# Two-layer RWKV-7/GLA decoder step: decays moved between the v tiles, the norm over heads in two token halves, identity products in the routings

## The chip, the cores and the metric

The kernel runs on one core of one Trainium2 chip. The metric is the device time of one execution in microseconds, as the median of several runs. Everything is float32 apart from a few bf16 0/1 matrices in the routing.

## The reference, cut to what matters

264 token rows (256 of a prompt, 8 samples of one token each) pass two layers. Layer 0 mixes with RWKV-7 (12 heads of 64), layer 1 with gated linear attention. Beside each mixer runs a small cross-attention to 256 memory tokens, and behind each a hierarchical mixture of 32 experts, of which each token uses two. The change concerns layer 0's mixer and the step from either mixer into its experts:

```python
w_log = -softplus(-(w0 + tanh(xw @ w1) @ w2)) - 0.5
decay = exp(-exp(w_log))
def step(S, inp):                       # per token; S is (head, value, key)
    sa = einsum('bhij,bhj->bhi', S, -kk_t)
    S = S * d_t[:, :, None, :] + sa[..., None] * b_t[:, :, None, :] + v_t[..., None] * k_t[:, :, None, :]
    return S, einsum('bhij,bhj->bhi', S, r_t)
mean = mean(y, -1); var = mean(square(y - mean), -1)     # per token and head
gn = ((y - mean) * rsqrt(var + GN_EPS)) * ln_g + ln_b
bonus = sum(r4 * k4 * r_k, -1) * v4
out = (gn + bonus) * g
...
x = x + mixed @ w_out
x = x + hier_moe(rms_norm(x, norm_ffn_g), ...)           # scores, top group, top 2 experts, SwiGLU experts
```

## The kernel before, in words

Each engine has its own program, and all order between engines is by semaphores that the code counts by hand. Within an engine the order is the order of the code. `link` makes an engine wait for its own instruction before the next; `mark` does this with a semaphore that others read as well (`t_dve`, `t_act`).

Layer 0's mixer (`mixer0` in each engine's program). The features stand on partitions, the tokens in columns, 128 features (two heads, a "pair") to a tile, six tiles to a vector. PE multiplies the input by the weights of r, k, v and of the low-rank gates, tile by tile, into two PSUM banks in turn; ACT copies each tile out (`out`). The last two weight chunks are those of r (`columns(4, ...)`) and of v (`columns(5, (512, 256))`, four and two tiles). After the v tiles PE sums r·k·r_k over each head (`head_sums(TT[0], 2)`), DVE forms the exclusive decay (`T2 = vL - vld`, L1828), ACT takes the exponentials into `TT[2]`, `TT[1]` and `TT[0]` (L1350 to L1354), DVE multiplies the head sums with v into `vld` (L1832) and scales r, kk, k and b (L1837 to L1840). `TT[2]` is also what the v products read, `TT[0]` what the head sums read. PE starts the scan at `T_SCALED`.

The scan handles 256 tokens as four chunks of 64, in two halves of two chunks. `scan_steps()` writes the order of its steps as a list, which PE, ACT and DVE all go through: each step is one group of 64x64 products into one of six banks (L857, L854), then one copy by ACT (L1379) or one masked copy or addition by DVE (L1883, names in `ON_DVE`). For each half a triangular matrix is inverted in steps (N, NT, X2, U1, ... U5); the chain (RHS, SA, Z, Y) then carries the state over the chunks, and Y's copy puts the scan's output into `vL`. The first half's chain lies among the second half's inversion; the second half's chain ends the scan. Between these, DVE updates the eight samples' states in 18 `sample_step`s (L1856 to L1872), one behind every second step of its own from the 16th on. Their result goes through memory (SP, L428 and L430) and comes back as `Dn[0]`, which PE transposes.

The norm over heads follows when the scan has ended and the samples are there: head sums of y (L767, six products of 264 columns into six banks), centring by DVE (L1916), square (L1918), head sums again, logarithm and exponential by ACT (L1387, L1388) for the inverse root, and five products or sums by DVE (L1920 to L1924) into `mixedT`. `t_dve` 9 ends it. SP waits for it and for the stored prompt state before it issues the first expert weights; the two chunks of `w_out` it has issued before.

`output` multiplies `mixedT` by `w_out` (L754), adds x by products with the identity (L757), forms router scores (L738) and transposes back (L742); `finish` is the second part for one tile. `route` on DVE then scales the scores, finds groups and experts, and builds one-hot matrices; PE counts ranks in between (L1154, L1159) and then gathers the tokens of the first four experts (L1064), whose units of 2 MB of weights it multiplies next (L1083). Weights run through a ring of eight units, in order, on SP's queue (L367); SP issues unit n when PE has used unit n - 8, units 6 and 7 of each layer when the two `w_out` halves are read.

Of the kernel before, what the change touches and what calls it, by code (L numbers as in the profile page):

```python
# [15 lines left out]
D = 1024  # L16
# [59 lines left out]
def scan_steps():  # L76
# [17 lines left out]
    return steps + fill + [(1, *c) for c in CHAIN]  # L94
# [3 lines left out]
SCAN = [st for st in STEPS if st[1] != "D"]  # L98
# [15 lines left out]
T_STATE_OUT = 4  # L114
# [21 lines left out]
T_MIXED = [9, 13]  # L136
OUT_STORES = [2, 4]
SEMS = """consts x_loaded norm_ss norm_h hT_ps hT gain_loaded router_w
# [14 lines left out]
def build(nc, A, O, dbg=None):  # L153
    with ExitStack() as ctx:
# [166 lines left out]
        Dn = [mixedT.rearrange("p k t -> p (k t)")[0:TS, TOK * n:TOK * (n + 1)] for n in range(2)]  # L321
        Dn += [h.rearrange("p t d -> p (t d)")[0:TS, TOK * n:TOK * (n + 1)] for n in range(4)]
        dscr = nc.dram_tensor("sample_vectors", [6, TS * TOK], F32, kind="Internal").ap()
# [46 lines left out]
        def _(sp):  # L370
# [32 lines left out]
            def mixer0():  # L403
# [26 lines left out]
                sp.dma_start(Dn[0], yscr.rearrange("(b c) -> b c", b=TS)).then_inc(s["dec_y"], 16)  # L430
                for i in range(2):
                    load_chunk(lambda b: [k3(b[:, 0:KT * 512], KT)], [A["w_out"][0].rearrange("(k p) n -> p k n", p=128)[:, :, 512 * i:512 * (i + 1)]])
# [167 lines left out]
        def _(pe):  # L600
# [128 lines left out]

            def output(l):  # L730
# [31 lines left out]
                finish(KT - 1)  # L762

            def head_sums(src, n):

                for q in range(PAIRS):
                    last = pe.matmul(ps[2 + q][:, 0:T], block64[:, :], src[:, q, :], start=True, stop=True)  # L767
                last.then_inc(s["sum_ps"], 1)

            def mixer0():  # L770
# [32 lines left out]
                columns(5, (512, 256))  # L803
                pe.wait_ge(s["t_dve"], 3)
                head_sums(TT[0], 2)

                def sample_rows(n):

                    src = (TT[2], vr, vk, vv, vkk, vb)[n]
# [51 lines left out]
                for st in STEPS:  # L861
                    if st[1] == "D":
                        sample_rows(st[2])
                    else:
                        scan_step(st)
                for st in SCAN[-BANKS:]:
                    wait_out(st)
                for q in range(PAIRS):
                    for u in range(2):
                        rows = slice(C * u, C * (u + 1))  # L870
                        last = pe.matmul(ps[2][rows, C * q:C * (q + 1)], cZ[rows, 0, q, :], ident[rows, rows], start=True, stop=True)
                last.then_inc(s["qn_ps"], 1)

                pe.wait_ge(s["dec_y"], 32)
                for q in range(PAIRS):
                    last = pe.transpose(ps[4][:, TS * q:TS * (q + 1)], Dn[0][:, 128 * q:128 * (q + 1)], ident[0:TS, 0:TS])
                last.then_inc(s["qn_ps"], 1)
                pe.wait_ge(s["t_act"], T_STATE_OUT)
                pe.wait_ge(s["t_act"], 5)
                head_sums(vL, 3)  # L880
                pe.wait_ge(s["t_dve"], 8)
                head_sums(TT[1], 4)
                pe.wait_ge(s["t_dve"], 9)

            def mixer1():
# [164 lines left out]
                for q in range(PAIRS):  # L1050
                    if q == 0:
                        pe.wait_ge(s["t_dve"], 10)
# [88 lines left out]
            for l in range(DEPTH):  # L1141
# [18 lines left out]
                last.then_inc(s["rank_ps"], 1)  # L1160

# [51 lines left out]
        def _(act):  # L1213
# [113 lines left out]
            def mixer0():  # L1327
# [17 lines left out]
                for dst in (vr, vv):  # L1345
                    for q in range(PAIRS):
                        out(dst[:, q, :], 128)

                act.wait_ge(s["t_dve"], 4)
                act.activation(TT[2][:, 0:PAIRS, TP:T], vld[:, :, TP:T], ACT.Exp)  # L1350
                act.activation(TT[2][:, 0:PAIRS, 0:TP], TT[2][:, 0:PAIRS, 0:TP], ACT.Exp)
                act.activation(TT[1][:, 0:PAIRS, 0:TP], vL[:, :, 0:TP], ACT.Exp).then_inc(s["t_act"], 1)
                act.wait_ge(s["t_dve"], 5)
                act.activation(TT[0][:, 0:PAIRS, 0:TP], vL[:, :, 0:TP], ACT.Exp, scale=-1.0).then_inc(s["t_act"], 1)  # L1354
# [4 lines left out]
                for st in STEPS:  # L1359
                    half, name, hf = st  # L1360
                    c = 2 * half + hf
                    if name == "D":
# [3 lines left out]
                        last.then_inc(s["qn"], 1)  # L1366
                    elif name not in ON_DVE:
# [13 lines left out]
                act.copy(cKn[:, 0], ps[2][:, 0:384].rearrange("p (q n) -> p q n", q=PAIRS)).then_inc(s["t_act"], 1)  # L1381
                act.wait_ge(s["qn_ps"], 9)
                act.copy(vL[:, :, TP:T], ps[4][:, 0:TS * PAIRS].rearrange("p (q b) -> p q b", q=PAIRS)).then_inc(s["t_act"], 1)

                act.wait_ge(s["sum_ps"], 4)
                for q in range(PAIRS):
                    link(act.activation(TT[1][:, q, :], ps[2 + q][:, 0:T], ACT.Ln, scale=1.0 / 64, bias=cst[:, 2:3]))  # L1387
                act.activation(TT[1][:, 0:PAIRS, :], TT[1][:, 0:PAIRS, :], ACT.Exp, scale=-0.5).then_inc(s["t_act"], 1)  # L1388
# [174 lines left out]
        def _(dve):  # L1563
# [209 lines left out]
            def mixer0():  # L1773
# [53 lines left out]
                dve.wait_ge(s["pj_out"], 43)  # L1827
                mark(dve.tensor_tensor(T2[:, :, 0:TP], vL[:, :, 0:TP], vld[:, :, 0:TP], ALU.subtract), "t_dve", 4)  # L1828
                dve.wait_ge(s["sum_ps"], 2)
                dve.wait_ge(s["t_act"], 2)  # L1830
                for q in range(PAIRS):
                    link(dve.tensor_tensor(vld[:, q, :], ps[2 + q][:, 0:T], vv[:, q, :], ALU.mult))  # L1832
                mark(dve.memset(sq[:, 0:1], 0.0), "t_dve", 5)
                dve.wait_ge(s["t_act"], 3)
                pc = slice(0, TP)
                link(dve.tensor_copy(lam[:, :, :], T1[:, :, C - 1:TP:C]))
                link(dve.tensor_tensor(vr[:, :, pc], vr[:, :, pc], T1[:, :, pc], ALU.mult))  # L1837
                link(dve.scalar_tensor_tensor(out=vkk[:, :, pc], in0=vkk[:, :, pc], scalar=-1.0, in1=T2[:, :, pc], op0=ALU.mult, op1=ALU.mult))
                link(dve.tensor_tensor(vk[:, :, pc], vk[:, :, pc], T0[:, :, pc], ALU.mult))
                mark(dve.tensor_tensor(vb[:, :, pc], vb[:, :, pc], T0[:, :, pc], ALU.mult), "t_dve", 6)  # L1840
# [33 lines left out]

                done_d, sampled = 0, 0
                for st in SCAN:
                    half, name, hf = st
                    if name not in ON_DVE:
# [26 lines left out]
                    mark(last, "c_dve", c_at(st))  # L1905
                    done_d += 1
# [7 lines left out]
                dve.wait_ge(s["sum_ps"], 3)  # L1914
                for q in range(PAIRS):
                    link(dve.scalar_tensor_tensor(out=T0[:, q, :], in0=ps[2 + q][:, 0:T], scalar=-1.0 / 64, in1=vL[:, q, :], op0=ALU.mult, op1=ALU.add))  # L1916
                mark(dve.memset(sq[:, 0:1], 0.0), "t_dve", 7)
                mark(dve.tensor_tensor(T1, T0, T0, ALU.mult), "t_dve", 8)  # L1918
                dve.wait_ge(s["t_act"], 6)
# [177 lines left out]
```

## Time and profile before

| what | value |
|---|---|
| three timed runs | 1717.71, 1719.99, 1725.26 us; median 1719.99 |
| profiled execution | 1716.36 us, span 1714.3 us |
| PE, DVE, ACT busy | 75%, 24%, 14% of the span |
| mean granted TensorE clock | 0.847 of full speed |
| DMA | 463.62 MB, mean 270 GB/s |

```profile
PEclk9968889897888998798998889779698888786686
DMA  9410202043659999999999823318399999999994
```

The span is cut into 40 slices of 42.9 us. A digit is a slice's mean in tenths: of the TensorE clock that was granted, and of the busy share of the 16 DMA engines. The two long runs of 9 in the second line are the experts of the two layers.

### The profile page before, as it was taken

The page shows a single profiled execution, that of the slowest core. Times are in us where ns is not written, and L with a number is a line of the kernel's source. Part 1 is how long each engine was busy: PE and PEld are TensorE (multiplying, and loading weights), DVE is VectorE, ACT ScalarE, POOL GpSimd, SP SyncE. Part 2 cuts the span into 40 slices and gives each one's busy share as a digit, 9 for nine tenths or more (in the row PEclk, how much of TensorE's full clock was granted, in tenths as well). Part 3 has the DMA queues.
Part 4 walks back from the last instruction along what each step waited for, and adds up shares of the span by engine and source line. Part 5 has one row for each costly group of instructions (what it writes and reads, how often), then busy time and mean ns, then how long its engine had stood idle before and what let it go on. Part 6 is the DMA issues. An engine that isn't in the chain of part 4 may idle for free.

```text
span 1714.3 us, 20945 instructions
## 1 busy us (share of the span) xinstructions
PE 1289.6 (75%) x9284; PEld 695.7 (41%) x9284; DVE 412.4 (24%) x824; ACT 246.4 (14%) x653; POOL 18.0 (1%) x53
## 2 busy tenths in 40 slices
PE   2968967775796775696675799879788665969774
PEld 1556757774651221332131466548433211514311
DVE  4044645853211110110110232430211011011013
ACT  2110322121210000010000222412100000101001
POOL 1000000000000000000000000000000000000000
PEclk9968889897888998798998889779698888786686
DMA  9410202043659999999999823318399999999994
GB/s 301 135 50 25 74 1 46 3 139 140 257 231 409 409 409 409 408 409 409 409 409 401 260 76 87 128 44 338 139 410 409 409 409 408 408 409 409 409 409 173
DMA packets 147457, 463.62 MB, mean 270 GB/s; under 512 B 12850, under 2 KB 37188, under 8 KB 147164
## 3 DMA queue, kind: packets, MB, share of 16 engines
q1 hardware_dynamic: 145964, 457.78, 69.3%
q0 software_dynamic: 1392, 4.38, 0.8%
q8 instruction: 77, 1.26, 0.3%
q14 instruction: 24, 0.20, 0.0%
HBM read 455.12 MB, written 7.02 MB: 270 GB/s over the span
## 4 chain that ended last, share of the span: by engine, by line
PE 48%; DMA 34%; DVE 9%; issue 3%; ACT 3%; SPq 3%; DVEq 0%; ACTq 0%
DMA slot<-in_exp_w_up 23%; PE bank L1083 9%; PE bank L1064 7%; PE bank L640 6%; DMA arena<-in_exp_w_up 6%; DMA slot<-in_exp_w_down 6%; PE bank L754 4%; PE bank L857 3%; PE bank L898 3%; PE bank L904 3%; SPq L367 2%; PE bank L1094 2%; PE bank L726 1%; PE bank L659 1%; DVE arena L1883 1%
## 5 line engine op out<-in xcount | busy, mean ns | idle before, releaser
L1083 PE MATMUL bank<-slot,hT 128*32 128x512 f32 x1536 | 238.4, 741 | 127.7 <-DMA slot<-in_exp_w_up 127.6
L1083 PEld LDWEIGHTS bank<-slot,hT 128*32 128x32 f32 x1536 | 49.9, 125 | 301.3 <-DMA slot<-in_exp_w_up 172.4
L1668 DVE SCALAR_TENSOR_TENSOR mixedT<-mixedT,bank 128x512 f32<-128x512 f32 x16 | 11.0, 687 | 523.9 <-ACT mixedT L1238 523.9
L1083 PE MATMUL bank<-slot,mixedT 128*32 128x512 f32 x768 | 100.0, 664 | 35.5 <-DMA slot<-in_exp_w_down 28.7
L1083 PE MATMUL bank<-arena,hT 128*32 128x512 f32 x512 | 83.9, 732 | 39.0 <-DMA arena<-in_exp_w_up 39.0
L1064 PE MATMUL bank<-arena,h 128*128 128x128 f32 (+1 forms) x384 | 100.7, 411 | 14.2 <-DVE arena L1661 10.0
L1094 PE MATMUL bank<-mixedT,arena 128*128 128x512 f32 (+1 forms) x192 | 89.9, 611 | 12.7 <-ACT mixedT L1247 12.7
L1064 PEld LDWEIGHTS bank<-arena,h 128*128 128x128 f32 (+1 forms) x384 | 76.4, 268 | 44.1 <-issue 22.4
L1238 ACT ACTIVATE mixedT<-bank 128x512 f32<-128x512 f32 x16 | 9.6, 597 | 534.1 <-PE bank L1083 534.1
L754 PE MATMUL bank<-mixedT,slot 128*128 128x264 f32 x256 | 63.8, 405 | 18.1 <-issue 18.1
L1064 PE MATMUL bank<-gain,h 128*128 128x128 f32 (+1 forms) x384 | 74.7, 328 | 0.0
L1680 DVE TENSOR_TENSOR x<-bank,x 128x512 f32<-128x512 f32 (+1 forms) x96 | 66.0, 687 | 36.0 <-PE bank L1094 36.0
L1083 PEld LDWEIGHTS bank<-slot,mixedT 128*32 128x32 f32 x768 | 24.2, 119 | 106.4 <-issue 52.5
L1064 PEld LDWEIGHTS bank<-gain,h 128*128 128x128 f32 (+1 forms) x384 | 57.0, 204 | 25.0 <-issue 12.3
L640 PE MATMUL bank<-slot 128*128 128x264 f32 x288 | 64.7, 386 | 0.6 <-ACT arena L1277 0.6
L1674 DVE COPY mixedT<-bank 128x512 f32<-128x512 f32 x16 | 11.1, 692 | 221.9 <-PE bank L1083 221.9
L1233 ACT ACTIVATE hT<-bank,gainT 128x128 f32<-128x128 f32 x128 | 36.6, 368 | 175.4 <-PE bank L1064 175.4
L754 PEld LDWEIGHTS bank<-mixedT,slot 128*128 128x128 f32 x256 | 50.0, 201 | 27.3 <-DVE mixedT L1924 16.6
L1094 PEld LDWEIGHTS bank<-mixedT,arena 128*128 128x128 f32 (+1 forms) x192 | 28.2, 160 | 77.2 <-issue 77.2
L640 PEld LDWEIGHTS bank<-slot 128*128 128x128 f32 x288 | 54.6, 190 | 10.3 <-ACT arena L1277 1.0
L1083 PEld LDWEIGHTS bank<-arena,hT 128*32 128x32 f32 x512 | 17.9, 122 | 92.9 <-issue 49.4
L1083 PE MATMUL bank<-arena,mixedT 128*32 128x512 f32 x256 | 40.2, 757 | 11.1 <-ACT mixedT L1244 6.0
(433 smaller groups left out, 1452.8 us busy)
## 6 DMA issues: line engine op xcount, KB each, us to landing
slot<-in_exp_w_up SPq DMA_DIRECT2D x96, 2048.0 KB, 24.0
slot<-in_exp_w_down SPq DMA_DIRECT2D x48, 2048.0 KB, 23.9
arena<-in_exp_w_up SPq DMA_DIRECT2D x32, 2048.0 KB, 23.6
arena<-in_exp_w_down SPq DMA_DIRECT2D x16, 2048.0 KB, 23.6
slot<-in_w_in SPq DMA_DIRECT2D x6, 1536.0 KB, 7.3
slot<-in_w_out SPq DMA_DIRECT2D x4, 2048.0 KB, 11.5
slot<-in_w_in SPq DMA_DIRECT2D x3, 2048.0 KB, 7.9
slot<-in_w_in SPq DMA_DIRECT2D x5, 1024.0 KB, 5.6
```

The source lines that it names most:

```text
L367: sp.dma_start(ring[buf], src.rearrange("e p n -> p e n")).then_inc(sem, 16)
L640: last = pe.matmul(p[0:m, 0:n], w(k), rhs(k), start=(k == 0), stop=(k == kt - 1))
L659: last = pe.matmul(ps[4 + m][:, :], mem[:, m, 128 * k:128 * (k + 1)], w[:, k, :], start=(k == 0), stop=(k == KT - 1))
L754: pe.matmul(p[:, 0:T], buf[:, 512 * i + 128 * b:512 * i + 128 * (b + 1)], mixedT[:, i, :], start=(i == 0), stop=False)
L857: last = pe.matmul(out, lt(c)[rows, q, :], rh(c)[rows, q, :], start=(i == 0), stop=(i == len(MM[name]) - 1))
L898: last = pe.matmul(p[0:m, 0:T], w(k)[:, c0:c0 + m], rhs(k), start=(k == 0), stop=(k == kt - 1))
L904: last = pe.matmul(p[:, 0:384], hT[:, k, 128 * t:128 * (t + 1)], w[:, k, :], start=(k == 0), stop=(k == KT - 1))
L1064: last = pe.matmul(ps[bank][:, 128 * (k % 4):128 * (k % 4 + 1)], h[0:m, t, 128 * k:128 * (k + 1)], G[par][0:m, t, :], start=(t == 0), stop ...
L1083: last = pe.matmul(ps[bank + half][rows, :], lhs[:, rows], ring[buf][:, e, half * FF:(half + 1) * FF], start=first, stop=last_)
L1094: return pe.matmul(ps[SC_BANK[o]][0:m, :], ST[:, c:c + m], yq[:, FF * n:FF * (n + 1)], start=True, stop=True)
L1233: last = act.activation(xs[par][:, k, :], ps[bank][:, 128 * (k % 4):128 * (k % 4 + 1)], ACT.Copy, scale=gainT[:, KT * l + k:KT * l + k + 1])
L1680: return dve.tensor_tensor(xt, ps[SC_BANK[o]][0:m, :], xt, ALU.add)
```

## The change

- **Decays.** The exponentials get buffers of their own in `h` and `hT`, which are free by then (`decay_ex`, `decay_in`); the third uses `TT[1]`. The subtraction and the exponentials are put between the copies of the v tiles, the head sums before the last two v tiles, and the products with v last.
- **Norm over heads.** The first 128 tokens are handled in the scan at two new places ("G", 0) and ("G", 1), into buffers in `wch[0]`; the other 136 after it. Sums of three pairs share a bank. The square moves from DVE to ACT. ln_g, ln_b, gate and bonus are folded into `vld` and `vg` by three products behind (0, "NT", 1). The samples' result comes back into two other buffers and is taken up before the state's transposes; the second `w_out` chunk is loaded when the first half's norm has left `wch[0]` (`t_dve` 8).
- **Identity products.** In both layers PE issues 41 products of the identity with itself behind the last `finish` and 5 behind the rank products.

```diff
+    after = steps.index((0, "Y", 1)) + 3
+    steps.insert(after, (1, "G", 0))
+    last_copy = max(n for n, st in enumerate(steps) if st[0] == 1 and st[1] not in ON_DVE and st[1] != "G")
+    steps.insert(last_copy + 1, (1, "G", 1))
...
+WARM = (41, 5)
...
                 for i in range(2):
+                    if i == 1:
+                        sp.wait_ge(s["t_dve"], 8)
...
+            def idle_products(count):
+                for n in range(count):
+                    pe.matmul(ps[n % 2][:, 0:128], ident[:, :], ident[:, :], start=True, stop=True)
...
                 finish(KT - 1)
+                idle_products(WARM[0])
...
-                columns(5, (512, 256))
+                columns(5, (512,))
                 pe.wait_ge(s["t_dve"], 3)
                 head_sums(TT[0], 2)
+                columns(5, (256,))
...
+                    elif st == (1, "G", 0):
+                        pe.wait_ge(s["qn"], 7)
+                        wait_out((0, "Y", 1))
+                        half_sums(vL[:, :, 0:HALF], 0)
+                    elif st == (1, "G", 1):
+                        pe.wait_ge(s["t_dve"], 7)
+                        pe.wait_ge(s["t_act"], 4)
+                        half_sums(gy2, 0)
...
                 last.then_inc(s["rank_ps"], 1)
+                idle_products(WARM[1])
...
# ACT
+                for q in range(PAIRS):
+                    out(vv[:, q, :], 128)
+                    if q == 1:
+                        act.wait_ge(s["t_dve"], 4)
+                        act.activation(decay_ex[:, :, TP:T], vld[:, :, TP:T], ACT.Exp)
+                        act.activation(decay_ex[:, :, 0:TP], decay_ex[:, :, 0:TP], ACT.Exp)
+                    if q == 2:
+                        act.activation(decay_in[:, :, 0:TP], vL[:, :, 0:TP], ACT.Exp).then_inc(s["t_act"], 1)
+                    if q == 3:
+                        act.activation(TT[1][:, 0:PAIRS, 0:TP], vL[:, :, 0:TP], ACT.Exp, scale=-1.0).then_inc(s["t_act"], 1)
...
+                    elif st == (1, "G", 0):
+                        act.wait_ge(s["t_dve"], 7)
+                        act.activation(gy2, gy, ACT.Square).then_inc(s["t_act"], 1)
+                    elif st == (1, "G", 1):
+                        act.wait_ge(s["sum_ps"], 4)
+                        for n in range(2):
+                            link(act.activation(grs[:, 3 * n:3 * n + 3, :], ps[n][:, 0:3 * HALF].rearrange("p (q t) -> p q t", q=3), ACT.Ln, scale=1.0 / 64, bias=cst[:, 2:3]))
+                        act.activation(grs, grs, ACT.Exp, scale=-0.5).then_inc(s["t_act"], 1)
...
# DVE
+                def scaled_out(cols, y, rstd):
+                    link(dve.tensor_tensor(y, y, rstd, ALU.mult))
+                    link(dve.tensor_tensor(y, y, vg[:, :, cols], ALU.mult))
+                    link(dve.tensor_tensor(mixedT[:, 0:PAIRS, cols], y, vld[:, :, cols], ALU.add))
...
+                    if st == (1, "G", 0):
+                        dve.wait_ge(s["sum_ps"], 3)
+                        centered(gy, 0, slice(0, HALF))
+                        mark(dve.memset(sq[:, 0:1], 0.0), "t_dve", 7)
...
+                    if st == (0, "NT", 1):
+                        link(dve.tensor_tensor(vld, vld, vec(V_LB), ALU.add))
+                        link(dve.tensor_tensor(vld, vld, vg, ALU.mult))
+                        link(dve.tensor_tensor(vg, vg, vec(V_LG), ALU.mult))
+                    if st == (1, "Z", 0):
+                        dve.wait_ge(s["t_act"], 5)
+                        scaled_out(slice(0, HALF), gy, grs)
+                        mark(dve.memset(sq[:, 0:1], 0.0), "t_dve", 8)
...
+                dve.wait_ge(s["sum_ps"], 5)
+                late = slice(HALF, T)
+                centered(T0[:, :, late], 2, late)
+                mark(dve.memset(sq[:, 0:1], 0.0), "t_dve", 9)
+                dve.wait_ge(s["t_act"], 9)
+                scaled_out(late, T0[:, :, late], T1[:, :, late])
+                mark(dve.memset(sq[:, 0:1], 0.0), "t_dve", T_MIXED[0])
```

## Rows read from the trace of the kernel before

**Rows 1.** Windows: us, busy by engine (x instructions), granted clock, DMA share, GB/s.

```profile
480.00:485.50 5.50, 5.50 (x22) 4.15 (x24) 0.00 (x0) 0.00 (x0) 0.00 (x0) 0.50 0.00 0
501.00:509.00 8.00, 8.00 (x48) 6.19 (x47) 1.37 (x2) 1.64 (x5) 0.00 (x0) 1.00 1.02 410
490.00:945.00 455.00, 322.62 (x1972) 115.39 (x1964) 51.31 (x77) 31.25 (x87) 0.00 (x0) 0.88 1.02 406
```

**Rows 2.** Timeline of SP, 486 to 490: start, duration, engine, line, operation, tiles.

```profile
488.88 0.37 SPq L367 DMA_DIRECT2D slot<-in_exp_w_down  x1
```

**Rows 3.** Timeline of the scan's preparation; idle before and its end in brackets.

```profile
213.03 1.81 DVE L1826 TENSOR_TENSOR slot<-slot,vecT 128x1584 f32<-128x1584 f32 x1
...
231.85 2.83 PE L767 MATMUL bank<-slot,block 128*128 128x264 f32 x12
232.05 0.39 ACT L1277 ACTIVATE arena<-bank 128x264 f32<-128x264 f32 x1 [3.17 <-PE bank L640]
...
234.34 0.24 ACT L1350 ACTIVATE slot<-slot 128x48 f32<-128x48 f32 x1 [1.90 <-DVE slot L1828]
234.49 1.47 ACT L1351 ACTIVATE slot<-slot 128x1536 f32<-128x1536 f32 x1
...
237.46 2.77 DVE L1832 TENSOR_TENSOR slot<-bank,arena 128x264 f32<-128x264 f32 x6 [3.15 <-ACT slot L1352]
...
242.18 1.76 DVE L1837 TENSOR_TENSOR arena<-arena,slot 128x1536 f32<-128x1536 f32 x1
...
249.37 2.83 PE L857 MATMUL bank<-arena 64*64 64x64 f32 x48 [14.69 <-DVE arena L1840]
```

**Rows 4.** Timeline of DVE early in the scan.

```profile
267.12 1.26 DVE L1883 TENSOR_TENSOR arena<-bank,dstrict 128x384 f32<-128x384 f32 x2 [9.53 <-PE bank L857]
```

**Rows 5.** Timeline of the scan's second half, ACT and DVE.

```profile
347.57 0.48 ACT L1379 COPY slot<-bank 128x384 f32<-128x384 f32 x1 [0.22 <-PE bank L857]
...
349.02 2.29 DVE L1868 TENSOR_TENSOR slot<-slot 96x2048 f32<-96x2048 f32 x1
...
351.58 0.56 DVE L1883 TENSOR_TENSOR arena<-bank,arena 128x384 f32<-128x384 f32 x1 [0.27 <-PE bank L857]
...
366.77 0.48 ACT L1379 COPY h<-bank 128x384 f32<-128x384 f32 x1 [4.60 <-PE bank L857]
```

**Rows 6.** The chain that ended last, behind the scan: start, us, what.

```profile
383.03 0.49 ACT slot L1379
...
385.42 2.92 PE bank L767 x12
...
393.22 4.42 PE bank L767 x12
397.66 0.49 ACT slot L1387
...
400.73 1.28 ACT L1388
402.02 1.53 ACT slot L1388
...
411.02 1.82 DVE mixedT L1924
```

**Rows 7.** DMA issues: operation, count, KB each, median us to landing.

```profile
out_prompt_rwkv_S<-slot POOLq DMA_DIRECT2D x2, 96.0 KB, 2.5
```

**Rows 8.** Timeline of PE between output and ranks, layer 0.

```profile
468.71 0.21 PE L1154 MATMUL bank<-arena,before_h 128*128 128x32 bf16 x1 [8.94 <-DVE arena L1631]
```

**Rows 9.** The chain that ended last: first gathers of both layers, a later one, units.

```profile
470.48 15.05 PE bank L1064 x48
...
500.82 8.46 PE bank L1064 x48
511.25 7.12 PE bank L1083 x64
...
1213.51 15.06 PE bank L1064 x48
```

**Rows 10.** Groups of PE by form, 1199.6 to 1200.58: count, busy us, mean ns.

```profile
L757 PE MATMUL bank<-ident,x 128*128 128x128 f32 x4 | 0.6, 274 | 0.0
```

More of the change, by code:

```diff
@@ L113 @@
 SAMPLE_AT = 16
-T_STATE_OUT = 4
+T_STATE_OUT = 7
+HALF = 128
+REST_T = T - HALF
 REST = {"pe": ["xg", "ST_ps", "up", "actT_ps", "down"] + [f"sc{o}" for o in range(6)],
@@ L135 @@
 RQ = 3
-T_MIXED = [9, 13]
+T_MIXED = [10, 14]
 OUT_STORES = [2, 4]
+WARM = (41, 5)
 SEMS = """consts x_loaded norm_ss norm_h hT_ps hT gain_loaded router_w
@@ L767, in head_sums, with half_sums @@
                     last = pe.matmul(ps[2 + q][:, 0:T], block64[:, :], src[:, q, :], start=True, stop=True)
+                last.then_inc(s["sum_ps"], 1)
+            def half_sums(src, bank):
+                w = src.shape[2]
+                for q in range(PAIRS):
+                    last = pe.matmul(ps[bank + q // 3][:, w * (q % 3):w * (q % 3 + 1)], block64[:, :], src[:, q, :], start=True, stop=True)
                 last.then_inc(s["sum_ps"], 1)
@@ L867, in mixer0 @@
                     wait_out(st)
+                pe.wait_ge(s["dec_y"], 48)
+                for q in range(PAIRS):
+                    last = pe.transpose(ps[7][:, TS * q:TS * (q + 1)], ybuf[q // 3][:, 128 * (q % 3):128 * (q % 3 + 1)], ident[0:TS, 0:TS])
+                last.then_inc(s["qn_ps"], 1)
+                pe.wait_ge(s["t_act"], 6)
+                half_sums(vL[:, :, HALF:T], 2)
                 for q in range(PAIRS):
@@ L870, in mixer0 @@
                         rows = slice(C * u, C * (u + 1))
-                        last = pe.matmul(ps[2][rows, C * q:C * (q + 1)], cZ[rows, 0, q, :], ident[rows, rows], start=True, stop=True)
+                        last = pe.matmul(ps[6][rows, C * q:C * (q + 1)], cZ[rows, 0, q, :], ident[rows, rows], start=True, stop=True)
                 last.then_inc(s["qn_ps"], 1)
[L874 to L883, printed above, removed]
+                pe.wait_ge(s["t_act"], 8)
+                half_sums(TT[1][:, 0:PAIRS, HALF:T], 4)
+                pe.wait_ge(s["t_dve"], T_MIXED[0])
             def mixer1():
@@ L1344, in mixer0 @@
                 act.activation(vL, vL, ACT.Exp, scale=-0.5, bias=cst[:, 3:4]).then_inc(s["t_act"], 1)
[L1345 to L1354, printed above, removed]
+                for q in range(PAIRS):
+                    out(vr[:, q, :], 128)
+                act.wait_ge(s["shift_stored"], 32)
+                for q in range(PAIRS):
+                    out(vv[:, q, :], 128)
[7 more added lines that the diff above has]
+                        act.activation(TT[1][:, 0:PAIRS, 0:TP], vL[:, :, 0:TP], ACT.Exp, scale=-1.0).then_inc(s["t_act"], 1)
                 act.wait_ge(s["shift_stored"], 32)
@@ L1366, in mixer0 @@
                         last.then_inc(s["qn"], 1)
+                    elif st == (1, "G", 0):
[3 more added lines that the diff above has]
+                        act.wait_ge(s["sum_ps"], 4)
+                        for n in range(2):
+                            link(act.activation(grs[:, 3 * n:3 * n + 3, :], ps[n][:, 0:3 * HALF].rearrange("p (q t) -> p q t", q=3), ACT.Ln, scale=1.0 / 64,
+                                                bias=cst[:, 2:3]))
+                        act.activation(grs, grs, ACT.Exp, scale=-0.5).then_inc(s["t_act"], 1)
                     elif name not in ON_DVE:
@@ L2004, in mixer1 @@
                                                         op0=ALU.mult, op1=ALU.mult)
-                mark(last, "t_dve", 10)
+                mark(last, "t_dve", 11)
                 dve.wait_ge(s["go_out"], PAIRS)
-                for n in range(11, T_MIXED[1] + 1):
+                for n in range(12, T_MIXED[1] + 1):
                     mark(dve.memset(sq[:, 0:1], 0.0), "t_dve", n)
```

74 lines of the change are left out of this document (39 added, 35 removed).

## The prediction

> **What bounds the kernel now.** I read the chain of waits first, then timelines of the stages that the diff touches, and last windows for clock and transfers. From the start of the scan's preparation to layer 0's experts the chain is one serial string of small PE, ACT and DVE steps. From then on the expert weights bound both layers: between 490 and 945 us the queues move 406 GB/s, which is all they reach [rows 1], while PE idles between units. That stream stands still ahead of each layer's first expert unit: eight units fill the ring, and the next transfer is issued only when PE has used the first, at 488.88 us [rows 2]. So each microsecond by which PE gets there sooner moves the restart, and with it the end of the layer, by a microsecond. The same holds in layer 1. The reader should see three stretches in which little else than the chain moves: the preparation of the scan (17.3 us after the last v copy), the norm over heads (29.3 us after the last copy of the scan), and the routing with the first gather at the low clock.
>
> **Decays between the v tiles.** Now the last v copy starts at 232.05 and the scan's first product at 249.37, 14.69 us after PE's previous work [rows 3]. After the change the order is this. DVE ends the r·k products at 213.03 + 1.81 = 214.84; the subtraction (1.76, as row L1837) follows at once, since its output no longer lies in a buffer that the v tiles read, and ends at 216.7. ACT is free after the second v copy (the six end at 232.05 + 0.39 and are 3.56 apart, 3.17 of it idle, so the second ends at 218.2); the small and the large exponential (0.24 + 1.47) end at 219.9, before the third v tile is ready at 221.4. The second large one ends at 223.3, the third, behind the fourth copy, at 226.8. So no v copy is late. DVE does two products from 223.3 to 227.1 and two from there to 230.7. The head sums (2.83 on PE) now stand before the last two v tiles, so these end 2.83 later: fifth copy done at 231.7, sixth at 235.3. Of the six products with v (2.77 / 6 = 0.46 each) five are done by 233.2, the sixth runs from 235.4 to 235.8, and with the marker PE starts the scan at about 236.0. Gain 249.4 - 236.0 = **13.4 us**. Its cover is the 3.17 us of ACT idle in each tile and DVE's idleness; without cover it would cost 4 exponential or product durations again, so I bound the gain by 9 and 14.5 (the upper end because PE no longer rests long before the scan).
>
> **The scan.** Three products over 1584 elements go to DVE behind NT: 3 x 1.82 = 5.5 us, in a gap of 9.53 us before DVE's next step [rows 4]: nothing, with 4 us of cover left. The first half's norm is put in twice. At the first place PE gets six sums of 128 columns (2.92 x 128/264 = 1.4 us [rows 6]), DVE two centring steps (0.56 each, as its steps over 384 elements) and ACT a square (about 0.75, half of the 1.47 exponential over 1536 elements). The price is the order: ACT takes its instructions in turn, and the square waits for DVE, which reaches the centring only after its sample step at 349.02 + 2.29 = 351.3 [rows 5]. So the centring ends at 352.6 and the square at 353.4, and behind it stand the copies that ACT makes at this point; the one of W1, at 347.57, is the second of them and moves to about 353.9, PE's U4 follows 0.1 later, and DVE's U4, now at 351.58, starts at 355.2: 3.6 late. The last sample step and the chain behind it move along. At the second place ACT does two logarithms, a table load on either side and an exponential (about 4.5 us) while it now idles 4.60 us before the copy at 366.77, and DVE's three scaling steps (3 x 0.93) fall into its wait during the last chunk. PE's second six sums mostly fall into the same wait. I take **4 us lost**; bounds 1.4 (only PE's sums count) and 9 (the whole 4.5 us of ACT comes on top).
> On the table loads the trace shows 1.28 us and the next activation 0.01 us behind it [rows 6]. The Trainium skill (ScalarE: Activation LUTs, "What ACT_TABLE_LOAD costs") gives 1.28 us and a drain of about 1.38 more per switch; the row shows no drain. By the page the scan would lose some 2.8 us more and the sum would be about 39; I go by the row.
>
> **The norm behind the scan.** Now: copy at 383.03 ends at 383.52, two short copies, sums 2.92, six centring steps, square, sums 4.42, six logarithms of 0.49, table load 1.28, exponential 1.53, five products of 1.82, end at 412.84 [rows 6]: 29.3 us. After, counted from 383.5: transposes of the sample rows and their copy 1.1; sums over 136 columns 1.5 (2.92 x 136/264); centring two steps of about 0.6 and marker, to 4.0; square on ACT 0.9; sums 1.6; two logarithms of 0.5 (the table load before them falls into the sums); table load 1.28; exponential 0.85; three products of 0.95 (1.82 x 816/1584), each hand-over 0.05 to 0.1: 13.0. Gain **16.3 us**, bounds 13 (sums at half clock as in the 4.42 row, loads exposed) and 18. The state's store on POOL's queue, for which SP waits ahead of the stream, is issued about 9 us before this ends and lands in 2.5 [rows 7]; the second half of the output's weights, now behind the first half's norm, is issued some 20 us before and read 20 us after. Neither is last.
>
> **Identity products in the routing.** PE idles 8.94 us before the ranks in layer 0 [rows 8], and its granted clock is at 0.50 (1.2 GHz) through the whole gather, 15.05 us, against 8.46 us for the same 48 records when it is at 1.00 (2.4 GHz) [rows 1, 9]. The change fills the gap with 41 products of 128x128 by 128. The nearest row is PE's product of the same shape with the identity in the output stage: four records in 0.6 us of which one takes 0.274 [rows 10], so (0.6 - 0.274) / 3 = 0.109 a record, and two records a product: 41 x 0.218 = 8.9 us. It fits to within 0.1. The five behind the ranks take 1.1 us, and PE now waits about as long there for DVE's one-hot. So they cost nothing at 0.218 apiece; the other bound is the gather at 0.50, 15.05 / 24 = 0.627 apiece. I take the former, since shape and clock are the same. The gain per layer: gather 15.05 - 8.46 = 6.6; the first unit now ends 488.88 - 485.53 = 3.4 after the gather [rows 2, 9], and at the full clock takes 16 records of 7.12 / 64, 1.8: another 1.6. **8.2 us** in layer 0, the same in layer 1, whose gather took 15.06: 16.4. Bounds 0 and 17 if the products cost nothing.
>
> **Sum.** 13.4 - 4 + 16.3 + 16.4 = 42.1 us. The profiled execution took 1716.36 us (span 1714.3), so 1674.3; the median of the three timed runs, 1719.99, lies 3.6 above it. I predict 1676, between the sum from the one and from the other.
>
> **Rivals.**
> (1) The products run but the clock isn't held through ranks and gather. For it: the gather keeps PE busy for 5.50 of 5.50 us and the clock stays at 0.50 [rows 1], so being busy alone didn't lift it; and the ranks are short products with a wait on either side. Against: once at 1.00, the same gather kept it there for 8 us [rows 1]. Time: 13.4 - 4 + 16.3 = 25.7 less, about 1691. The Trainium skill (TensorE: Matmul & The Clock Gate, "What's actually happening") says that activity releases the throttle; by that rule products without gaps are enough and this rival falls, but the row above shows busy time that didn't do it.
> (2) Slower: the identity products run at the gather's low-clock pace, 0.627 each. Then the ranks start 41 x 0.627 - 8.94 = 16.8 us late and the gather 3.1 - 1.0 = 2.1 more, in both layers, and the gather gains nothing: 37.8 - 25.7 = 12.1 slower, 1728. It decides from 2 x (41p - 8.94) > 25.7, a product of more than 0.53 us. Against: the output's last products run at the full clock's pace [rows 10], and the first identity product follows them at once.
> (3) The scan pays more: the square's wait and the second place's ACT work both come last, 9 to 13 us instead of 4, 1681 to 1685. For it: DVE idles 0.27 us where it now takes U4; against: 4.6 us of ACT idle [rows 5].
> (4) The earlier layer 0 is swallowed by the weight stream. Against: the stream stands still until 488.88, so this only decides if units 6 and 7, which wait for the output's weights, came late; it would cost the first few us, about 1685.
>
> **How the numbers follow.** Forecast within 1668 to 1684: 0.62. Rival 1 (1691): 0.13. Rival 3 beyond 1684, 4 and like mishaps (1684 to 1700): 0.13. Faster than 1668 (first unit and output start warmer): 0.06. Rival 2: 0.04; of the rest, 0.02, half lies near no change. The range takes the forecast, rival 1 and most of rival 3: 1666 to 1693. A difference of 0.5%, 8.6 us, is about what a measurement tells from none: faster 0.93, same 0.03, slower 0.04.
>
> **What would show it.** Scan's first product 4 us or less after the last v copy; DVE's U4 of the second half some 3 to 4 us later relative to the scan's start; about 13 us from the scan's last copy to the output's first product's release; granted clock 1.00 in the gathers, which last 8.5 us; first ranks product within 0.3 us of DVE's last routing step. Wrong, if a gather shows 0.50, if PE still works on identity products when the ranks' input is ready, or if the scan is over 9 us longer.

## The result and the profile after

The changed kernel takes 1670.55 us (median of four runs, 1663.65 to 1673.67) against 1721.65 for the kernel before on the same chip; the ratio is 0.970 [0.967, 0.973]. Its profiled execution took 1672.15 us, span 1670.2, which is 44.1 less than the span before; the medians lie further apart, by 51.1. PE is busy for 77% of the span, at a mean granted clock of 0.872.

The preparation of the scan, timeline of PE, ACT and DVE (answers to [rows 3]):

```profile
231.70 0.39 ACT L1314 ACTIVATE arena<-bank 128x264 f32<-128x264 f32 x1 [3.17 <-PE bank L656]
232.19 0.43 DVE L1890 TENSOR_TENSOR slot<-bank,arena 128x264 f32<-128x264 f32 x1 [2.29 <-ACT arena L1314]
...
232.80 1.61 PE L887 MATMUL bank<-arena 64*64 64x64 f32 x48 [1.14 <-DVE arena L1891]
```

The scan's first product starts 1.1 us after the last v copy, where it was 17.3. It starts 16.6 us sooner; 3.2 of these were there already after 80 us and 3.0 where the changed code begins, so the decays gave 13.4 to 13.5. The first step takes 1.61 us instead of 2.83: PE's granted clock is 1.00 in the scan's first 10 us, where it was 0.83.

The middle of the scan, around the first place of the norm (answers to [rows 5]; L1919 a sample step, L1930 centring, L1409 the square, L1428 the copies behind it, L887 the products of U4 behind those, L1950 DVE's step of U4):

```profile
329.38 2.29 DVE L1919 TENSOR_TENSOR slot<-slot 96x2048 f32<-96x2048 f32 x1
...
331.70 1.15 DVE L1930 SCALAR_TENSOR_TENSOR slot<-bank,slot 128x384 f32<-128x384 f32 x2
332.92 0.06 DVE L1944 MEMSET arena<- 128x1 f32 x1
333.01 0.84 ACT L1409 ACTIVATE slot<-slot 128x768 f32<-128x768 f32 x1 [6.54 <-DVE arena L1944]
333.76 1.98 ACT L1428 COPY slot<-bank 128x384 f32<-128x384 f32 x5
334.65 1.08 PE L887 MATMUL bank<-slot,arena 64*64 64x64 f32 x24 [2.83 <-ACT slot L1428]
...
335.84 0.56 DVE L1950 TENSOR_TENSOR arena<-bank,arena 128x384 f32<-128x384 f32 x1 [2.87 <-PE bank L887]
```

ACT idles 6.54 us for the square's input, five copies are queued behind it, and PE stands still for 2.83 us. U4 of the second half starts at 335.84, 15.7 us sooner than before [rows 5], although the scan started 16.6 sooner and its steps ahead of this place had gained up to 3.1 more, 1.55 of them in its first 120 records. Yet the whole scan is not longer but 2.3 us shorter: 131.3 us from its first to its last product instead of 133.6.

The norm behind it, the chain that ended last (start, us, what; answers to [rows 6]):

```profile
364.13 0.49 ACT slot L1428
...
365.65 1.67 PE bank L796 x12
...
369.71 1.67 PE bank L796 x12
...
371.40 0.61 ACT slot L1437
...
372.66 1.28 ACT L1439
373.94 0.01 issue
373.95 0.89 ACT slot L1439
...
377.02 1.02 DVE mixedT L1936
```

From the copy's end, 364.62, to the norm's end at 378.16 it is 13.5 us instead of 29.3.

The routing of layer 0, the same view, and windows (answers to [rows 9] and [rows 1]; L749 the identity products in two records each, L1190 ranks, L1100 gather):

```profile
425.60 9.16 PE bank L749 x82
434.75 0.23 PE bank L1190 x6
...
435.25 1.31 PE bank L749 x10
436.56 8.24 PE bank L1100 x48
...
1176.75 8.24 PE bank L1100 x48
```

```profile
446.72 0.37 SPq L380 DMA_DIRECT2D slot<-in_exp_w_down  x1
```

```profile
436.50:442.00 5.50, 5.50 (x34) 4.29 (x33) 3.11 (x14) 1.14 (x4) 0.00 (x0) 1.00 0.01 3
447.00:903.00 456.00, 330.82 (x1980) 121.78 (x1972) 51.32 (x77) 31.24 (x87) 0.00 (x0) 0.86 1.02 405
```

The gather runs at the full clock. SP issues the first transfer behind the full ring at 446.72, 42.2 us sooner than at [rows 2], and the stream then moves what it moved before, 405 GB/s. Layer 1 shows the same (gather 1176.75, 8.24 us).

### The profile page after: what moved, and what is told of

The parts are those of the page before. It is cut to its first block, busy times and chain, and to the rows that moved or that the text cites. A ratio compares the mean times of both kernels' runs of the same rounds, so it can differ in the third digit from the quotient of the medians.

```text
span 1670.2 us, 21379 instructions
## 1 busy us (share of the span) xinstructions
PE 1282.9 (77%) x9492; PEld 702.9 (42%) x9492; DVE 412.9 (25%) x828; ACT 249.4 (15%) x656; POOL 18.0 (1%) x53
## 3 DMA queue, kind: packets, MB, share of 16 engines
q8 instruction: 78, 1.28, 0.3%
## 4 chain that ended last, share of the span: by engine, by line
PE 47%; DMA 38%; DVE 7%; SPq 3%; issue 2%; ACT 2%; DVEq 0%; ACTq 0%
DMA slot<-in_exp_w_up 26%; PE bank L1119 8%; PE bank L656 6%; DMA arena<-in_exp_w_up 6%; DMA slot<-in_exp_w_down 6%; PE bank L1100 5%; PE bank L775 4%; PE bank L887 4%; SPq L380 3%; PE bank L940 3%; PE bank L934 3%; PE bank L1130 2%; PE bank L749 1%; PE bank L742 1%; PE bank L675 1%
## 5 line engine op out<-in xcount | busy, mean ns | idle before, releaser
L1119 PE MATMUL bank<-slot,hT 128*32 128x512 f32 x1536 | 232.0, 723 | 133.8 <-DMA slot<-in_exp_w_up 133.8
L1119 PE MATMUL bank<-arena,hT 128*32 128x512 f32 x512 | 80.2, 707 | 40.8 <-DMA arena<-in_exp_w_up 40.8
L1100 PE MATMUL bank<-arena,h 128*128 128x128 f32 (+1 forms) x384 | 81.8, 351 | 12.1 <-DVE arena L1712 7.8
L1100 PEld LDWEIGHTS bank<-arena,h 128*128 128x128 f32 (+1 forms) x384 | 62.6, 222 | 37.3 <-issue 12.6
L1100 PE MATMUL bank<-gain,h 128*128 128x128 f32 (+1 forms) x384 | 74.8, 329 | 0.0
L1119 PEld LDWEIGHTS bank<-slot,mixedT 128*32 128x32 f32 x768 | 24.0, 119 | 110.6 <-issue 51.1
L1100 PEld LDWEIGHTS bank<-gain,h 128*128 128x128 f32 (+1 forms) x384 | 57.1, 204 | 25.0 <-issue 12.3
```

Source lines behind the costliest of these rows:

```text
L1100: last = pe.matmul(ps[bank][:, 128 * (k % 4):128 * (k % 4 + 1)], h[0:m, t, 128 * k:128 * (k + 1)], G[par][0:m, t, :], start=(t == 0), stop ...
L1119: last = pe.matmul(ps[bank + half][rows, :], lhs[:, rows], ring[buf][:, e, half * FF:(half + 1) * FF], start=first, stop=last_)
```

## Experiments

Each kernel below, by stage. "Scan": first product to end of the last; "tail": from there to the output's first product; "ranks": from the first rank product to SP's next transfer, layers 0 and 1. Times are medians; the ratio is to the kernel before in runs on the same chip, with its interval.

| kernel | us | ratio | scan | tail | ranks |
|---|---|---|---|---|---|
| before | 1721.65 | 1 | 133.6 | 30.9 | 20.2, 20.5 |
| changed | 1670.55 | 0.970 [0.967, 0.973] | 131.3 | 15.1 | 12.1, 12.1 |
| e1 no identity | 1683.53 | 0.979 [0.977, 0.981] | 132.2 | 15.1 | 20.2, 20.5 |
| e2 identity only | 1698.92 | 0.988 [0.986, 0.990] | 134.0 | 30.8 | 12.1, 12.1 |
| e3 old decays | 1682.94 | 0.979 [0.976, 0.981] | 134.4 | 15.1 | 12.1, 12.1 |
| e4 old norm | 1687.84 | 0.981 [0.978, 0.983] | 132.2 | 31.5 | 12.1, 12.1 |
| e5 no transfers | 1669.70 | 0.971 [0.969, 0.973] | 131.9 | 15.1 | 12.1, 12.1 |
| e6 square late | 1668.09 | 0.970 [0.968, 0.973] | 131.9 | 15.1 | 12.1, 12.1 |
| e7 e5 and e6 | 1663.95 | 0.967 [0.965, 0.970] | 126.7 | 15.1 | 12.1, 12.1 |
| e8 e4 and e5 | 1679.88 | 0.976 [0.974, 0.979] | 125.7 | 31.6 | 12.1, 12.1 |
| e9 e7, state in pieces | 1660.64 | 0.968 [0.965, 0.970] | 122.6 | 15.1 | 12.1, 12.1 |
| e10 identity doubled | 1687.51 | 0.982 [0.980, 0.985] | 131.6 | 15.1 | 12.1, 12.1 |
| e11 e7, identity in tail | 1661.42 | 0.967 [0.965, 0.969] | 127.1 | 15.1 | 12.1, 12.1 |
| e12 e9 and e11 | 1660.77 | 0.967 [0.965, 0.969] | 123.0 | 15.1 | 12.1, 12.1 |

Each stage is read from one profiled execution. Where no edit touched them, the tail and the ranks agree between kernels within 0.1 us and the scan within 0.9 (the changed kernel, e1 and e10 have the same scan and show 131.3, 132.2 and 131.6); the whole time differs by several us (last section). So a part is sized by its stage, and the medians are its check.

**e1: the identity products undone.**

```diff
-WARM = (41, 5)
+WARM = (0, 0)
```

> The changed kernel without its 41 and 5 identity products in each layer. Theory (the products hold PE's clock through ranks and gather, 8.2 us a layer): both first gathers last 15 us again, the median is some 16 us above the changed kernel's 1670.6, about 1687, 34 below the kernel before. Rival A (the clock would be held anyway, since the shorter norm leaves less rest ahead of the routing): gathers stay at 8.3, time 1671. Rival B (the first units hide the cold gather): gathers 15, time under 1676.

Both gathers run at the low clock again (0.50 granted). The chain of e1 in both layers:

```profile
437.26 15.06 PE bank L1100 x48
...
1183.88 15.06 PE bank L1100 x48
```

From the ranks to the restart it takes 8.1 and 8.3 us longer; the ratio is 0.009 above the changed kernel's, 15 us. The shorter norm alone leaves the clock low.

**e2: the kernel before with the identity products alone.** (Diff: `idle_products` and its two calls.)

> The kernel before with the identity products alone. Theory: gathers 8.3 instead of 15.05 us in both layers, ranks no later, stream restarts 8.2 us sooner in each layer: 16 us below the kernel before, about 1704. Rival: the products pay only together with the shorter norm (its clock carries over): gathers stay at 15, no difference, or slower where the products overrun the 8.94 us gap at a low clock (up to 12 slower).

The chain of e2 in layer 0:

```profile
468.93 8.24 PE bank L1071 x48
```

The gathers are at 8.24, the two stages 8.0 and 8.3 shorter, in a kernel whose norm and decays are the old ones: the parts add up. The median fell by more, 21 us, and the span of the profiled run by less, 12.4; the stages explain 16.4, and untouched stretches, which differ from run to run, make up the rest either way.

**e3: the decays undone.** (Diff: the blocks of `mixer0` on PE, ACT and DVE between the r tiles and the scan as they were.)

> The changed kernel with the decays back in the shared buffers behind the last v tile. Theory (decays worth 13.4 us, all on the path): the scan's first product again some 17 us behind the last v copy, the median 13.4 above the changed kernel's, about 1684. Rival A (the long rest of PE ahead of the scan costs clock in the scan's first steps, so it is worth more): first steps at 2.8 us instead of 1.6, 16 or more above, 1687. Rival B (given back later in the scan, because DVE's sample steps are then on time): less than 9 above.

The scan's first product is 14.68 us behind PE's last work again and its first step takes 2.82 us; the scan is 3.1 us longer. By stages the decays are worth 13.4 and some 3 behind them (rival A); the whole time shows 12 to 14, so it doesn't bear out the 3.

**e4: the norm undivided, decays and identity products kept.**

> The kernel before with the decays and the identity products, and the norm undivided behind the scan. Theory of the prediction (norm 16.3 gained in the tail, 4 lost in the scan): 12.3 above the changed kernel, 1683. Rival A (from the trace of the changed kernel, where the scan in fact came out shorter although its first-half norm is in it): the norm's pieces in the scan cost nothing at the end, 15.8 to 18 above, 1686 to 1689. What tells them apart is the scan's length in this run: about 4 us shorter than the changed kernel's 131.8 by the prediction, the same or longer by rival A.

The scan isn't shorter without the norm's pieces: 132.2 us against 131.3 to 132.2 in the kernels that have them (rival A). With 16.4 in the tail the norm's division is worth 16 to 17 us, as the median says (17.3). So the 4 us that the prediction had set against it were not to be seen, though PE visibly waits 2.83 us for the square. Where they went shows in the chain of e4 at the same place ("issue" is time in which the engine waits for nothing that the profile shows):

```profile
337.49 3.61 PE bank L867 x123
341.10 2.97 issue
```

PE stands still for 2.97 us in the midst of a step (123 records are five steps of 24 and three more), where it waits for no semaphore. The kernel before has the same 2.97 behind the same 123 records, and another 0.66 and 1.91 in the last chain:

```profile
353.56 3.61 PE bank L857 x123
357.17 2.97 issue
...
374.17 1.91 issue
```

Transfers of the kernel before over 351 to 357.1 and over the 3 us in which PE stands still (queue, kind: packets, MB, share):

```profile
q1 hardware_dynamic: 98, 1.52, 79.2%
```

```profile
q1 hardware_dynamic: 14, 0.05, 4.4%
q8 instruction: 1, 0.02, 2.1%
q14 instruction: 1, 0.01, 0.6%
```

The 98 packets are the store of the samples' state, in rows of 16 KB. While they pass, no packet of the kind "instruction" is moved; the next is moved when they end, and PE goes on. Hence a theory: PE had run out of instructions behind the store. Four kernels test it.

**e5: the changed kernel with no transfers in the scan's second half.**

```diff
-                sp.wait_ge(s["dec_sum"], 3)
-                sp.dma_start(O["sample_rwkv_S"]..., DS...)   # moved behind both w_out loads
+                sp.wait_ge(s["c_act"], c_at(SCAN[-1]))
                 for i in range(2):
```

> The changed kernel with the sample state's store and both halves of the output's weights issued only after the last copy of the scan (nothing is loaded or stored in the scan's second half). Theory (the price of the first half's norm was hidden because PE in any case stood still for its own instructions behind the sample state's store, 2.97 us in the kernel before; in the changed kernel that stall is already gone, it falls into the wait for the square): the scan stays at 131.3 us from its first to its last product, within 1; the time 1670 to 1672. Rival (transfers slow the second half in another way, or the norm costs nothing whatever is beside it): the scan 3 us shorter, or unchanged together with an unchanged one in the old-norm kernel with the same edit.

**e6: the changed kernel with the square behind ACT's last Vn copy.**

```diff
                     elif st == (1, "G", 0):
-                        act.wait_ge(s["t_dve"], 7)
-                        act.activation(gy2, gy, ACT.Square).then_inc(s["t_act"], 1)
+                        pass
...
                         act.copy(o, b).then_inc(s["c_act"], 1)
+                        if st == (1, "Vn", 1):
+                            act.wait_ge(s["t_dve"], 7)
+                            act.activation(gy2, gy, ACT.Square).then_inc(s["t_act"], 1)
```

> The changed kernel, ACT's first-half square moved behind its last Vn copy, so that no copy waits for DVE's centring. Theory of the prediction (the ACT order is the price, 3.6 us): U4 of the second half starts about 3 us sooner and the scan is about 3 us shorter, 1667. Rival (PE's stall on its instructions behind the state's store comes back as soon as PE isn't held up by the square): the chain shows PE idle for up to 3 us again some 5 us after the store was issued, the scan gets no more than 1 us shorter, 1670.

**e7: both. e8: the old norm of e4 with the edit of e5.**

> Both edits: the square late and no transfers in the scan's second half. If PE's stalls come from the transfers and the square's wait is the price of the norm, the two together give what neither gives alone: scan about 128 us instead of 131.3, time 1667 to 1668. If the norm has no price at all, 131 as before.

> The kernel with the old undivided norm (decays and identity products in), the state's store and the output's weights issued behind the scan. Theory (PE's 2.97 and 1.03 us without a cause in the chain are waits for instructions behind these transfers): both stalls vanish, the scan falls from 132.2 to about 128.2 us, the time by 4, to about 1684; then the norm's first half does cost 3 us in the scan, seen against the changed kernel with the same edit. Rival (PE waited there for DVE's step behind the sample reduction, which ends 0.18 us before PE goes on): the 2.97 stays, the scan at 131 or more.

Neither edit alone shortens the changed kernel's scan (131.9 both); both together do, to 126.7 (128 expected). In e6 ACT's copies are on time, and PE's standstill is back, in the chain at

```profile
337.59 3.26 PE bank L887 x111
340.85 2.76 issue
```

In e8 the scan falls by 6.5 us against e4, and neither of its standstills is in the chain. That is more than the 4.0 expected; behind them the granted clock in the scan's last stretch rose too. e4 from 346 to 368, then e8 from 343.5 to 359.6 (504 and 431 records, so the clocks can be compared and not the lengths):

```profile
346.00:368.00 22.00, 18.64 (x504) 17.73 (x500) 5.02 (x9) 2.84 (x7) 0.00 (x0) 0.87 0.54 194
```

```profile
343.50:359.60 16.10, 13.75 (x431) 13.06 (x426) 4.46 (x8) 2.41 (x6) 0.00 (x0) 1.00 0.02 5
```

That clock isn't a fixed price of the standstills: the kernel before has them and shows 1.00 from 366 to 383.

So the norm's pieces do have a price, 131.93 - 125.67 = 6.3 us with the square in the change's place (e5 against e8). With the square late it is 1.0 (e7 against e8), hardly more than equal scans differ by. The old norm had paid as much for its transfers, 6.5 us (e4 against e8); in the kernel before, the standstills at these places come to 2.97 + 0.66 + 1.91 = 5.5.

**e9: e7 with the samples' state loaded in eight pieces.** The theory says that the other standstill, 4.0 to 4.35 us in the first half of every scan so far, is the load of the same state.

```diff
-                sp.dma_start(DS.rearrange("p i j -> p (i j)"), A["state_rwkv_S"]...).then_inc(s["dec_in"], 16)
+                for n in range(8):
+                    cols = slice(512 * n, 512 * (n + 1))
+                    sp.dma_start(DS.rearrange("p i j -> p (i j)")[:, cols], A["state_rwkv_S"]...[:, cols]).then_inc(s["dec_in"], 16)
```

> The kernel with the square late and no transfers in the scan's second half, and the load of the sample state in the scan's first half (1.5 MB in rows of 16 KB, beside which PE stands still for 4.0 to 4.3 us without a cause in the chain, in every kernel so far) issued as eight loads of rows of 2 KB. Theory (PE's instructions wait behind the 16 KB packets): instruction packets are served among the small ones, the 4.2 us stall falls to 1 or less and the scan from 126.7 to 123 or 124 us; time about 1661. Rival A (it is the whole load that must pass, whatever its packets): the stall stays near 4. Rival B (the stall goes, but DVE's steps decide behind it): stall gone, scan still 126.

The chain of the changed kernel, and of e9, at that place:

```profile
246.64 10.18 PE bank L887 x344
256.82 4.04 issue
```

```profile
247.24 10.18 PE bank L890 x344
257.42 0.75 issue
```

The transfers, of the changed kernel from 251 to 257.5 and of e9 from 249 to 259:

```profile
q1 hardware_dynamic: 129, 1.39, 90.4%
```

```profile
q1 hardware_dynamic: 1447, 1.71, 59.2%
...
q8 instruction: 2, 0.03, 1.3%
```

Behind the same 344 records 4.04 becomes 0.75 (1.34 in e12, which has this edit too), and one packet of q8, at 255.64, passes among the 2 KB ones. The scan is 4.1 us shorter than e7's, and the loaded bytes are the same. That the packets of q8 are PE's the profile doesn't say; it follows from their number and timing. The changed kernel has 78 of them for 18984 products and weight loads of PE, one for each 243. And each time that PE stands still for over 0.6 us and its next product waits for no semaphore, 24 times in the scans of these fourteen kernels, it goes on 1.2 to 1.5 us behind the end of a packet of q8. Left open is what helped in e9, as its load is not only in smaller packets but also in eight pieces that keep the engines less busy. Small packets alone are not enough: the 1.91 of the kernel before comes beside `w_out`, in rows of 2 KB (before, 369 to 374.2):

```profile
q1 hardware_dynamic: 908, 1.83, 95.7%
```

The Trainium skill (Runtime: NRT & Kernel Launch, "Instruction fetch mechanics") tells of such a supply, refilled in blocks of 16 KiB by DMA while the engine works on, and calls its cost mostly hidden; the packets here are of that size, and in this kernel the cost is not hidden where large packets share the engines.

**e10: 82 identity products instead of 41.**

> The changed kernel with 82 instead of 41 identity products behind the output in each layer. Theory (41 fit the 8.94 us of PE's idle time at 0.218 each and so cost nothing; the cover is used up): the ranks start 41 x 0.218 = 8.9 us later in each layer, the rest is the same: some 18 us above the changed kernel, about 1688. Rival A (there is more cover, since the ranks wait for something later than DVE's last step): less than 5 a layer. Rival B (a product costs more than 0.218 when they run on): over 10 a layer, 1691 and above.

From the output's last product with `w_out` to the ranks it takes 21.1 us instead of 12.0 in both layers, 9.16 more each, or 0.223 a product; the ratio is 0.012 higher, 21 us, the median 17. The 41 used all the cover that there is.

**e11: e7 with 33 identity products while PE waits for the norm's end.**

> The kernel with the square late and no transfers in the scan's second half, and 33 identity products on PE while it waits 7.8 us for the norm's end ahead of the output. Theory (PE's rest there costs clock: the output's first tile takes 5.71 us for 16 records, the next 3.83): 33 x 0.218 = 7.2 fit, the first tile takes 3.8 to 4, the output starts no later, 1.9 us gained, about 1662. Rival A (the clock isn't held, as the products follow sums that ran with waits between): first tile 5.7, no gain. Rival B (they overrun, at the low clock 0.44 each or more): the output starts up to 7 late, 1667 to 1671.

e7, then e11, from 378 to 384:

```profile
378.00:384.00 6.00, 6.00 (x24) 4.87 (x24) 0.00 (x0) 0.39 (x1) 0.00 (x0) 0.77 0.62 225
```

```profile
378.00:384.00 6.00, 6.00 (x30) 5.14 (x29) 0.00 (x0) 0.39 (x1) 0.00 (x0) 1.00 0.52 180
```

The output's first tile takes 3.80 us instead of 6.41 in e7 (5.71 in the changed kernel), and the output 41.5 instead of 44.1; the tail is the same 15.1. The time's difference to e7, 2.5 us, is within what runs differ by, and it was measured on another chip.

**e12: e9 and e11 together.**

> The changed kernel with the four edits together: square late, no transfers in the scan's second half, the sample state's load as eight loads of 2 KB rows, and 33 identity products in the norm's tail. If they don't meet each other, the scan stays at 122.6 us, the output at 41.5, and the time is 1660.6 - 2.5 = 1658, about 12.5 below the changed kernel and 62 below the one before. If they do (the sooner scan leaves the output's weights to land behind the end of the norm), 1661.

Each stage is as in its own experiment (123.0, 41.5), so the edits don't meet; the time, 1660.77, is no better than e9's. Its profiled run reached layer 1's output 1.8 us sooner than e9's and ended 2.3 later, in stretches that no edit touches. It beats the kernel before, as e9 and e11 do. Against the changed kernel the stages of the three are shorter and their medians 9 to 10 us lower, but the intervals of the ratios overlap; and which of the three is best these runs can't tell.

## Why the prediction was right, step by step

- **Decays, 13.4 predicted:** 13.4. No v copy came late, and the sum's last term (sixth product with v, marker, first step) is the row at 232.80. Not in the sum was that the first steps run at the full clock when PE hasn't rested: this gave the 1.55 us of the scan's first 120 records; e4, which has the new decays and the old norm, has a scan 1.5 shorter than the kernel before.
- **Scan, 4 us lost predicted; 2.3 gained** (1.4 to 2.7, as equal scans differ). This is the step that failed. "The price is the order" was right and even low: 6.3 us by e5 and e8, of which 131.9 - 126.7 = 5.2 go when the square moves (the prediction had 3.6 for it). Wrong was to add that price to the scan as it stood. The scan before held 2.97, 0.66 and 1.91 us of standstill beside transfers. In the changed kernel the state's store begins to pass while PE waits for the square, the second chunk of `w_out`, which now waits for the first half's norm, begins only 4.2 us before the scan's end, and the chain shows no standstill at either. One loss took the place of the other. The standstills stood in the chain of waits as "issue", and the prediction did not ask whether they would stay; its bounds, 1.4 to 9, allowed no gain.
- **Norm tail, 16.3 predicted:** 15.8 by the table. Sums 1.67 (1.5 and 1.6 predicted), centring 0.59 each, square 0.89, table load 1.28, exponential 0.89 (0.85), three products 1.02 each (0.95). The lower bound of 13 took the 4.42 us row of the kernel before for sums at half clock; the clock granted there was 0.66.
- **Identity products, 8.2 a layer predicted:** 8.0 and 8.3. They took 9.16 us instead of 8.9, and the gather 8.24 instead of 15.05.
- **Sum.** The stages give 13.4 + 2.3 + 15.8 + 8.0 + 8.3 = 47.8 against 42.1 predicted; the scan's term, 6.3 off, is the whole of the difference. The span fell by 44.1, since untouched stretches took 3.7 back (3.2 won at the start, 6.2 lost in layer 1's mixer, 0.7 lost elsewhere). So the profiled run lies near the forecast in part by luck: what the scan gained against it, the mixer of layer 1 lost. The median, 1670.55, is 5.5 below the 1676 forecast.
- **Rivals.** (1) fell: the clock is 1.00 in the gather, and e1 and e2 show that the products alone decide it, with the norm and the decays old or new. (2) fell: 0.223 a product, far from 0.53; e10 shows the cover that it turned on is real, and that it is used up. (3) fell: the price, 6.3 us, lies between the 4 of the forecast and the 9 to 13 of the rival, and the scan didn't become longer by it. (4) fell: the stream kept its 42 us to the end of layer 0.
- **The table load.** The next activation starts 0.01 us behind the 1.28 (373.94), in the changed kernel too. The Trainium skill (ScalarE: Activation LUTs, "What ACT_TABLE_LOAD costs") adds a drain of about 1.38; no run here shows it.
- **The clock.** In e1 PE rests for 8.9 us ahead of the ranks, and the gather behind them, 48 records without a gap, takes 15.06 us at a granted clock of 0.50. With identity products in that rest the same records run at 1.00. The Trainium skill (TensorE: Matmul & The Clock Gate, "What's actually happening") has activity release the throttle. The gather behind identity products agrees with it; the one in e1, busy from end to end and still at 0.50, does not.

## What to carry to other kernels

Before a stall is priced, look at what the chain shows as idle without a cause at the same place: a new wait that falls into an old one is free, and takes its price back when the old one goes. An instruction whose input comes late belongs behind those that are ready in its engine's order; moving one square on ACT was worth 5.2 us, once nothing else held PE there. Identity products in idle time of PE keep its clock for what follows, as long as they fit: 41 were free, 82 cost 9.2 us a layer.

## What was not expected of the hardware

- **Transfers keep instructions out.** While 1.5 MB pass in rows of 16 KB, no packet of q8 moves until the last of them, and PE stands still for 2.8 to 4.35 us in the midst of a step, unless it waits for something else in that time. As eight loads in rows of 2 KB the same load costs 0.75 us (e9) or 1.34 (e12); `w_out`, in rows of 2 KB, cost 0.66 and 1.91 in the kernel before.
- **The same code, another clock.** From layer 0's last expert unit to layer 1's output, which no edit touches, the profiled runs took 207.3 us (before), 213.5 (changed), 209.8 (e10) and 216.0 (e7), with the granted clock at 0.83, 0.80 and 0.79 in the first, second and last:

```profile
948.60:1155.80 207.20, 182.53 (x788) 110.42 (x789) 71.98 (x173) 58.28 (x150) 2.09 (x2) 0.83 0.40 121
```

```profile
905.40:1118.90 213.50, 188.75 (x789) 113.47 (x789) 72.00 (x173) 58.28 (x150) 2.09 (x2) 0.80 0.39 118
```

```profile
904.00:1120.00 216.00, 191.24 (x789) 114.42 (x789) 72.03 (x173) 58.22 (x150) 2.09 (x2) 0.79 0.38 116
```

DVE and ACT are busy for the same time in all three, so it is PE's clock that differs. These are single executions, and those of one kernel spread as widely (e4: 1681.18 to 1692.10 us), so the difference need not lie in the kernels. What sets the clock there stays open; it hides gains of 2 us, as of e11 and e12.
